# Gate products two iterations sooner, three pieces taken tile by tile, sums of squares on GpSimd

## What is computed

```python
for i in range(2):
    h = rmsnorm(x, g0) * (1 + scale) + shift
    y = short_conv_mixer(h) if i == 0 else ssd_mixer(h)
    x = x + gate * rmsnorm(y, g1)
    h = rmsnorm(x, g2) * (1 + scale) + shift
    x = x + gate * rmsnorm(swiglu_ffn(h), g3)
```

## Time and profile before

| what | value |
|---|---|
| median of 3 runs | 3520.47 us (3519.66 to 3521.72) |
| the profiled execution: its time, its span | 3519.32 us, 3517.4 us |
| mean granted TensorE clock | 0.950 of full speed |
| busy, share of the span | PE 86%, DVE 61%, ACT 40%, POOL 17% |
| HBM traffic over the span | 226 GB/s |

### The profile page before, as it was taken

How to read it: one execution, slowest core, us unless ns; L and a number is a source line. 1 busy time by engine, 2 the same in 40 slices (tenths; PEclk the granted TensorE clock), 3 DMA queues, 4 the chain that set the end, 5 groups by cost and what they waited for, 6 DMA issues and landing times.

```text
span 3517.4 us, 34727 instructions
## 1 busy us (share of the span) xinstructions
PE 3008.4 (86%) x12066; PEld 2079.7 (59%) x12066; DVE 2138.0 (61%) x3994; ACT 1399.4 (40%) x2882; POOL 599.3 (17%) x540
## 2 busy tenths in 40 slices
PE   5999999799777889999888978987879787777777
PEld 4867888587555668888667864465546432223222
DVE  6655443677555544443255479988777979755555
ACT  3233222344444542222472245775434333333333
POOL 0000000000000000000000003334444354443442
PEclk9999999899888999999999989999989999999999
DMA  6544444244111324443220449898999999999998
GB/s 222 181 143 126 144 141 136 76 142 128 37 36 36 102 81 147 140 149 118 97 90 13 166 178 350 302 357 347 407 420 419 355 414 421 421 421 421 421 421 345
DMA packets 147549, 797.84 MB, mean 227 GB/s; under 512 B 16304, under 2 KB 18480, under 8 KB 81712
## 3 DMA queue, kind: packets, MB, share of 16 engines
q0 software_dynamic: 73728, 536.90, 37.6%
q1 hardware_dynamic: 69840, 251.69, 22.0%
q10 hardware_dynamic: 3808, 7.02, 0.6%
HBM read 793.46 MB, written 2.10 MB: 226 GB/s over the span
## 4 chain that ended last, share of the span: by engine, by line
PE 52%; DMA 19%; DVE 19%; ACT 6%; issue 3%; POOL 0%; DVEq 0%; SPq 0%; ACTq 0%; POOLq 0%
PE psum L153 52%; DMA tail<-in_experts,tail 19%; DVE tail L187 4%; DVE tail L170 2%; ACT L164 2%; DVE arena L182 2%; ACT arena L164 2%; DVE tail L182 2%; DVE tail L193 1%; DVE tail L190 1%; DVE region L170 1%; ACT tail L164 1%; DVE tail L196 1%; DVE tail L205 1%; DVE arena L170 1%
## 5 line engine op out<-in xcount | busy, mean ns | idle before, releaser
L153 PE MATMUL psum<-tail,arena 128*128 128x256 f32 (+2 forms) x3580 | 1267.3, 503 | 266.5 <-ACT arena L164 236.2
L153 PE MATMUL psum<-rounded,rounded 128*128 128x512 f32 x5496 | 1321.0, 401 | 99.9 <-ACT arena L164 58.4
L153 PEld LDWEIGHTS psum<-rounded,rounded 128*128 128x128 f32 x5496 | 1051.1, 193 | 345.5 <-ACT arena L164 61.4
L153 PEld LDWEIGHTS psum<-tail,arena 128*128 128x128 f32 x3580 | 674.2, 198 | 813.8 <-issue 756.7
L216 POOL DMA_INDIRECT tail<-in_experts,tail x512 | 581.5, 1136 | 1760.9 <-DVE tail L199 864.6
L187 DVE CUSTOM_DVE_ANT_0 tail<-tail 128x1024 f32<-128x1024 f32 x512 | 621.1, 1224 | 307.0 <-DMA tail<-in_experts,tail 305.5
L164 ACT ACTIVATE tail<-tail 128x1 f32<-128x1 f32 (+1 forms) x1056 | 266.4, 252 | 780.0 <-DVE tail L187 742.6
L170 DVE TENSOR_TENSOR rounded<-arena,rounded 128x1024 fp32r<-128x1024 f32 (+2 forms) x285 | 316.5, 1111 | 364.6 <-ACT rounded L164 364.4
L164 ACT ACTIVATE rounded<-arena 128x1024 fp32r<-128x1024 f32 (+2 forms) x317 | 291.7, 939 | 446.2 <-DVE arena L170 238.9
L153 PE MATMUL psum<-arena 128*128 128x1 f32 (+3 forms) x792 | 201.1, 378 | 77.3 <-ACT arena L164 37.6
L164 ACT ACTIVATE arena<-psum 128x256 f32<-128x256 f32 (+2 forms) x210 | 97.6, 481 | 407.2 <-PE psum L153 406.4
(11 more groups left out here) (82 smaller groups left out, 1483.9 us busy)
## 6 DMA issues: line engine op xcount, KB each, us to landing
arena<-in_ada SPq DMA_DIRECT2D x136, 512.0 KB, 3.9
arena<-in_fin SPq DMA_DIRECT2D x88, 512.0 KB, 4.2
arena<-in_win SPq DMA_DIRECT2D x56, 512.0 KB, 3.3
arena<-in_fout SPq DMA_DIRECT2D x32, 512.0 KB, 4.0
...
```

The costliest lines, as they stand in the source:

```text
L153: return self.e.matmul(o, a, b, start=start, stop=stop, skip_group_check=skip)
```

## The change

- **Mixer's loop**: z(kk) goes to TensorE in iterations 2kk+3 and 2kk+4, still ahead of part b; ACT's silu stands in iteration 2kk+4, after `act_ssd_b` and before part a; DVE's gate multiplication in 2kk+5, with a wait on its own skip term. The norm of group g moves from n = 4g+10 to n = 4g+8, its TensorE sum behind part b. Tiles 0 to 7 of the output are rounded in iterations 32 and 33, and only half a z piece is left after the loop.
- **Norms**: scaling and EPS go into ACT's Ln, which reads PSUM (`dve_rstd` goes, all over the kernel); the delta rule's q and k keep an addition on DVE.
- **Sums of squares**: `pool_out` adds the squares of tiles 0 to 6 on GpSimd into `ysum`, and TensorE does 2 sums per layer in place of 8; `pool_pair_sum` adds a group's two tiles, 1 sum in place of 2.
- **Boundaries**: the gain is applied in ACT's copy of y; DVE multiplies and adds in place. A third piece is prepared in `act_pre`/`dve_pre` (layers 1 to 3), and `pe_first` takes three pieces (two in layer 0) tile by tile, the third four tiles behind.
- **Step sizes**: DVE does one operation of the softplus per projection; the turning and the sums move from projection 4 and 6 to 24 and 26.

```diff
-def dve_rstd(e, name, last, n, r, width=512):
+def act_rstd(e, name, last, n, r, width=512):
...
-    e.ts(r, ps[name][:, 0:width], 1.0 / n, ALU.mult, EPS, ALU.add).then_inc(*ps.release(name))
-def act_rstd(e, name, r):
+    e.act(r, ps[name][:, 0:width], ACT.Ln, bias=cc("eps"), scale=1.0 / n).then_inc(*ps.release(name))
...
-    e.act(r, r, ACT.Ln).then_inc(*ln_ok.tick(name))
-    e.wait_ge(*ln_ok.at(name))
...
 def pe_pre(e, i):
...
 def act_pre(e, i):
+    if i:
+        act_ahead(e)
...
-    act_rstd(e, ("pre", i), rst[0])
+    act_rstd(e, ("pre", i), ("pre", i, 7), D, rst[0])
...
 def dve_pre(e, i):
-    dve_rstd(e, ("pre", i), ("pre", i, 7), D, rst[0])
+    if i:
+        dve_ahead(e)
...
+def pe_first(e, i, keys):
+    own = [ps.claim(key, ALL) for key in keys]
+    for k in range(8 + 4 * (len(keys) - 2)):
+        for u, key in enumerate(keys):
+            m = k - 4 if u == 2 else k
+            if 0 <= m < 8:
+                if m == 0:
+                    e.wait_ge(*ps.vacant(key))
+                pe_gemm(e, pc[key], own[u], hrhs, ready=h_at(i), own=[m])
+    for key in keys:
+        pe_after(e, pc[key], ALL)
 def pe_out(e, i, groups, rhs, ready, norm=True, behind_first=None):
...
-        if norm and kk:
-            pe_stat(e, ("post", i, kk - 1), stat, ones, kk == 1, False)
...
+        e.wait_ge(*sq.done(("post", i, 6)))
+        e.mm(stat, ones, ysum, True, False)
...
 def act_out(e, i, groups):
...
-        act_square(e, ("post", i, kk), ps["y", i, kk])
-        e.act(yT[:, kk, :], ps["y", i, kk], ACT.Copy).then_inc(*ps.release(("y", i, kk)))
-    act_rstd(e, ("post", i), rst[1])
+        if kk:
+            act_square(e, ("post", i, kk), ps["y", i, kk])
+        else:
+            e.act(ysum, ps["y", i, kk], ACT.Square).then_inc(*sq_ok.tick(("post", i, kk)))
+        if kk < 7:
+            act_y(e, i, kk)
+    act_rstd(e, ("post", i), ("post", i, 7), D, rst[1])
+    act_y(e, i, 7)
+def act_y(e, i, kk):
+    e.wait_ge(*der_ok.at((i, "post")))
+    e.act(yT[:, kk, :], ps["y", i, kk], ACT.Copy, scale=post(i, kk)).then_inc(*ps.release(("y", i, kk)))
...
 def dve_out(e, i, groups):
+    dve_derived_post(e, i)
...
-    dve_derived_post(e, i)
-    dve_rstd(e, ("post", i), ("post", i, 7), D, rst[1])
+    e.wait_ge(*rs_ok.at(("post", i)))
...
-            if k == 0:
-                e.wait_ge(*der_ok.at((i, "post")))
-                e.wait_ge(*rs_ok.at(("post", i)))
-            if k > 1:
-                e.wait_ge(*x_ok.at((i, k - 2)))
-            e.stt(gd[k % 2], yT[:, k, :], post(i, k), rst[1], ALU.mult, ALU.mult).then_inc(
-                *dve_b.tick(("post", i, k)))
+            e.wait_ge(*ps.done(("y", i, k)))
+            e.tt(yT[:, k, :], yT[:, k, :], rst[1], ALU.mult).then_inc(*y_sc.tick((i, k)))
...
-            e.wait_ge(*dve_b.at(("post", i, k - 1)))
-            e.tt(xT[:, k - 1, :], xT[:, k - 1, :], gd[(k - 1) % 2], ALU.add).then_inc(
-                *x_ok.tick((i, k - 1)))
+            e.wait_ge(*y_sc.at((i, k - 1)))
+            e.tt(xT[:, k - 1, :], xT[:, k - 1, :], yT[:, k - 1, :], ALU.add).then_inc(*x_ok.tick((i, k - 1)))
+def pool_out(e, i):
+    for kk in range(1, 7):
+        key = "post", i, kk
+        e.wait_ge(*sq_ok.at(key))
+        if kk > 1:
+            e.wait_ge(*sq.done(("post", i, kk - 1)))
+        e.tt(ysum, ysum, sq[key], ALU.add).then_inc(*sq.release(key))
...
 def pe_ffn(e, half):
-    for kk in range(KF):
-        for part in range(2):
+    pe_first(e, half, [("ffn", half, 0, 0), ("ffn", half, 0, 1), ("ffn", half, 1, 0)])
+    for kk in range(1, KF):
+        for part in range(1 if kk == 1 else 0, 2):
...
-            pe_gemm(e, pc[key], o, hrhs, ready=h_at(half) if kk == 0 and part == 0 else None)
+            pe_gemm(e, pc[key], o, hrhs)
...
 def act_ffn(e, half):
...
-        act_ahead(e)
+        if kk:
+            act_ahead(e)
...
-def pe_dt(e):
-    p = pc["dt"]
-    o = ps.claim("dt", ALL)
-    e.wait_ge(*ps.vacant("dt"))
-    pe_gemm(e, p, o, hrhs, ready=h_at(2))
-    pe_after(e, p, ALL)
-def softplus_dve(e, x, tmp3, ok, sig, tag):
+def softplus_steps(e, x, tmp3, ok, sig, tag):
...
     done(e.ts(u, w, 2.0, ALU.add))
+    yield
     done(e.recip(u, u))
+    yield
...
+def softplus_dve(e, x, tmp3, ok, sig, tag):
+    for _ in softplus_steps(e, x, tmp3, ok, sig, tag):
+        pass
 def act_dt(e):
-    act_ahead(e)
...
 def dve_dt(e):
-    dve_ahead(e)
...
-    softplus_dve(e, dtT, [a[0:32, :] for a in sp], dt_act.at("exp"), dt_dve, "dt")
+    yield from softplus_steps(e, dtT, [a[0:32, :] for a in sp], dt_act.at("exp"), dt_dve, "dt")
+    yield
...
+    yield
...
 def pe_xbc(e):
-    for n in range(32):
-        if n == 4:
+    pe_first(e, 2, ["dt", ("xbc", 0), ("xbc", 1)])
+    for n in range(2, 32):
+        if n == 24:
...
-        if n == 6:
+        if n == 26:
...
 def act_xbc(e):
...
-        if n == 4:
+        if n == 24:
...
-        if n == 6:
+        if n == 26:
...
 def dve_xbc(e):
+    steps = dve_dt(e)
...
+        next(steps, None)
...
 def pool_ssd(e):
-    for n in range(32):
-        g, c = ITS[n]
+    for n in range(33):
+        if norm_of(n) is not None:
+            pool_pair_sum(e, norm_of(n))
+        g, c = ITS[n] if n < 32 else (0, 3)
...
+    pool_pair_sum(e, 7)
...
 def pe_ssd_b(e, n):
...
 def pe_norm_pair(e, g, banks):
...
-    for u in range(2):
-        pe_stat(e, ("zn", g, u), o, ones, u == 0, u == 1)
+    e.wait_ge(*sq.done(("zn", g, 0)))
+    pe_stat(e, ("zn", g, 1), o, ones, True, True)
+def pool_pair_sum(e, g):
+    e.wait_ge(*sq_ok.at(("zn", g, 1)))
+    e.tt(sq["zn", g, 1], sq["zn", g, 1], sq["zn", g, 0], ALU.add).then_inc(*sq.release(("zn", g, 0)))
...
 def act_pair_squares(e, g):
...
 def dve_z(e, kk):
...
+    e.wait_ge(*ps.done(("sy", kk // 2, kk % 2)))
...
-def dve_pair_rstd(e, g):
-    dve_rstd(e, ("zn", g), ("zn", g, 1), 256, rst[g % 2])
...
-second_of = lambda n: (n - 6) // 2 if n > 5 and n % 2 == 0 else None
-silu_of = lambda n: (n - 7) // 2 if n > 6 and n % 2 else None
-norm_of = lambda n: (n - 6) // 4 - 1 if n > 9 and n % 4 == 2 else None
+second_of = lambda n: (n - 4) // 2 if n > 3 and n % 2 == 0 else None
+gate_of = lambda n: (n - 5) // 2 if n > 4 and n % 2 else None
+norm_of = lambda n: (n - 8) // 4 if n > 7 and n % 4 == 0 else None
...
+round_of = lambda n: range(4 * (n - 32), 4 * (n - 31)) if n >= 32 else ()
...
 def pe_ssd(e):
...
-        if n > 4:
-            pe_z(e, (n - 5) // 2, FRONT if n % 2 else BACK)
+        if n > 2:
+            pe_z(e, (n - 3) // 2, FRONT if n % 2 else BACK)
+        if n > 1:
+            pe_ssd_b(e, n - 2)
...
-        if n > 1:
-            pe_ssd_b(e, n - 2)
...
-    pe_z(e, 14, BACK)
-    pe_norm_pair(e, 6, RG)
-    pe_after(e, pc["z", 14], RG)
-    pe_z(e, 15, range(8))
+    pe_z(e, 15, BACK)
...
 def act_ssd(e):
...
-        if silu_of(n) is not None:
-            act_z(e, silu_of(n))
+        if second_of(n) is not None:
+            act_z(e, second_of(n))
...
-            act_rstd(e, ("zn", norm_of(n)), rst[norm_of(n) % 2])
+            act_rstd(e, ("zn", norm_of(n)), ("zn", norm_of(n), 1), 256, rst[norm_of(n) % 2])
...
+        act_o(e, round_of(n))
+    act_z(e, 15)
...
-    act_z(e, 14)
-    act_pair_squares(e, 6)
-    act_o(e, range(0, 4))
-    act_rstd(e, ("zn", 6), rst[0])
-    act_ahead(e)
-    act_z(e, 15)
+    act_o(e, range(8, 10))
...
-    act_o(e, range(4, 10))
-    act_rstd(e, ("zn", 7), rst[1])
-    act_o(e, range(10, 16))
+    act_o(e, range(10, 14))
+    act_rstd(e, ("zn", 7), ("zn", 7, 1), 256, rst[1])
+    act_o(e, range(14, 16))
...
 def dve_ssd(e):
...
-        if silu_of(n) is not None:
-            dve_z(e, silu_of(n))
-        if norm_of(n) is not None:
-            dve_pair_rstd(e, norm_of(n))
+        if gate_of(n) is not None:
+            dve_z(e, gate_of(n))
...
+        dve_o(e, round_of(n))
+    dve_z(e, 15)
...
-    dve_z(e, 14)
-    dve_pair_rstd(e, 6)
-    dve_o(e, range(0, 4))
-    dve_after(e, pc["z", 14])
-    dve_norm_pair(e, 6)
-    dve_ahead(e)
-    dve_z(e, 15)
...
-    dve_o(e, range(4, 10))
-    dve_pair_rstd(e, 7)
-    dve_o(e, range(10, 12))
+    dve_o(e, range(8, 14))
...
-    dve_o(e, range(12, 16))
+    dve_o(e, range(14, 16))
...
 def act_o(e, tiles_of):
...
+        e.wait_ge(*s_pe.at(31))
+        e.wait_ge(*s_ce.at(31))
...
 def dve_o(e, tiles_of):
...
-            act_rstd(e, ("rn", f, n // 2), rst[n // 2 % 2])
-        yield
-def dve_qkv(e, f):
-    for s in range(15):
-        n = s - 3
-        if 0 <= n < 8 and n % 2:
...
-            dve_rstd(e, ("rn", f, g), ("rn", f, g), 64, rst[g % 2])
+            act_rstd(e, ("rn", f, g), ("rn", f, g), 64, rst[g % 2])
+        yield
+def dve_qkv(e, f):
+    for s in range(15):
...
-            dve_rstd(e, ("dnn", f, g), ("dnn", f, g), 1.0, R4[g])
+            e.wait_ge(*sq.done(("dnn", f, g)))
+            e.ts(R4[g], ps["dnn", f, g], EPS, ALU.add).then_inc(*ps.release(("dnn", f, g)))
...
-    for g in range(2):
-        act_rstd(e, ("dm", f, g), rst[g])
```

(14 more changed lines are left out.)

48 lines of the change are left out of this document (27 added, 21 removed).

## The result

The changed kernel takes **3441.22 us** (median of 4 runs, 3437.34 to 3443.28), the kernel before 3520.06 beside it: ratio 0.9774, 95% interval 0.9757 to 0.9791. The forecast was 3438.0 in 3400 to 3476. Four or five runs of one kernel lie up to 12 us apart (3437.0 to 3448.7 in the widest case), so a difference of a few us between two medians is only used where a trace shows its place.

The account below looks back on a forecast made before the run. TensorE was taken as full in the projections, the mixer's loop as bound by waits between engines. Savings of 21.9, 5.8, 2.0, 3.5, 7.6, 32 and 8 sum to 81 us; 3519.3 less 81 gives 3438, range 3400 to 3476.

Parts of the forecast that it names:

- 1, sums: Output stages: six fewer TensorE sums of squares per layer at 0.91 us each, 21.9 us saved in four layers.
- 2 and 3, norms, x update, pieces: Layer boundaries and norms: shorter norm chains save 5.8 us, x update 2.0, three pieces tile by tile 3.5 (0 to 10).
- for the last stage itself I count nothing: Last stage: fewer DVE instructions, a few more ACT waits; no gain counted, bounded by 5 us either way.
- 4, step sizes: Projections: one step-size operation per projection; the third projection's 7.07 us wait shrinks; 7.6 us saved (4 to 11).
- 5, the loop: Mixer's loop: period falls from 41.0 to 35.5 us, 32 saved over six periods (18 to 45), 8 after the loop.
- The pair's sum: Mixer's loop: GpSimd's sum of a pair ends after part b's start, costing 0.4 us per period, inside TensorE's idling.
- A: Mixer's loop: all eight periods stay near 41 us, as ACT's queue and a low clock return the gain; 3470; chance 0.21.
- B: Mixer's loop becomes bound by TensorE, 27 to 29 us per period; 3393 us; chance 0.12.
- C: Output stages and norms: GpSimd's adds make it slower, 3563 us at 12 us per add; chance 0.05, other losses included.
- D: Whole kernel: nothing moves, the first block's gain is taken back before the gathers; 3519 us; chance 0.02.
- E: Mixer's loop: a further 1.3 us drain per ACT table load, 45 us in all; 3483 us; chance 0.01.
- The rule on VectorE and GpSimd: Mixer's loop: whichever starts first blocks the other; pair sum could hold DVE 1 to 2 us per period, some 11.

Follow-up runs that it names:

- both-first: Changed kernel with ACT, in the loop's even iterations, rounding the next state at the head and taking the gate's silu ahead of state copy and Exps: 3410.58 us.
- the runs with the rounding first: Changed kernel with ACT rounding the next position's state at the head of the loop's even iterations: 3421.53 us alone, 3410.58 with silu ahead, 3425.74 with silu last.

## Why the prediction was right, step by step

The range and the mechanisms held. That the total came within 3 us (78.8 measured, 81 in the sum) is partly luck: the sums gave 3 us less than forecast, the loop's end 2 less, norms with x update and pieces 5 more, step sizes 1 more, the loop up to S(32) 3 more, and the stages behind 1706 us took back 6.4 that weren't in the sum.

- **1, sums:** 21.9 forecast, 18.5 measured. GpSimd's adds of 1.3 us are hidden, as said. The price of a sum, 0.91 us from the difference of two pacings, was a little high: 6.32 - 5.45 = 0.87 where it stands, which with six per layer is 5.2. From first product to last sums the layers gained 4.0, 5.8, 4.8 (layer 2, from S(32)) and 4.0; why less than 5.2 in three of them isn't placed.
- **2 and 3, norms, x update, pieces:** 11.3 forecast. What the ledger leaves at the attention's first product is 84.3 - 18.6 (sums) - 8.6 (step sizes: 27.0 - 18.4) - 35.0 (S(2) to S(32)) - 6 = 16. Of these, 11.2 lie at the boundaries, where norms and x update work: layer 0's first product comes 2.2 sooner, and from the last sums of a layer to the next first product it is 1.6, 1.7, 2.6 and 3.1 us less (24.81 to 23.20, 23.10 and 22.24; 23.10 to 19.98 ahead of the attention). The forecast for them was 7.8. The form of the norm was put back at one boundary only, the last, and cost 0.3 us there. The other 4.9 lie inside the layers (2.0, 1.1 and 1.9 in layers 0, 1 and 3) and aren't placed. The step of part 3 that failed is the 3.5 us left after its own deductions: they were too small, and in layer 2 the later end of the step sizes' product makes a loss of it, 1.65 us.
- **What stands behind the layers**, inside part 2 and "for the last stage itself I count nothing": failed, and by the prediction's own sign. It was to be wrong if the stages after 1706 us were longer or shorter by more than the bound of 5; from the attention's first product to the end they took 1810.9 us and take 1817.3, 6.4 more. I counted 1.6 us of gain for four short chains and missed an owner: a bank that DVE had freed at once is now freed by ACT, late in its queue. By the medians the new form of these norms cost 6.7 us; by the trace 4.1 behind the first gather (1516.1 less 1512.0) and 1.0 ahead of it. Some 1 of the 1.9 us that the attention stage lost stays unexplained.
- **4, step sizes:** 7.6 forecast, 8.6 in the ledger, 6.7 in the run; waits 1.37 and 1.05 for 1.7 and 1.4. The credit for the pieces within it (1.5) was wrong in sign (-1.65).
- **5, the loop:** forecast 11.9, 7.65, 9.3, 5.9; measured 11.07, 7.75, 9.07, 5.90. Six periods 32 forecast, 37.2 in the ledger, 36.7 by two runs that differ in the order alone. By its own periods the sum would have 6 x 5.5 = 33 where it has 32. What was high is n%4 = 0. Its beginning lost 2.2 us where I had none. End of the loop: 8 forecast, 6 to 7 measured.
- **The pair's sum:** 0.4 us per period forecast, nothing measured in this order, where TensorE idles anyway. In the order of before it cost 14 us.
- **Rivals.** A is out: no period stays near 41. B did not happen, but the runs that reorder ACT's queue show that much of it was to be had: both-first takes 30.2 us per period (181.07/6) against B's 27 to 29 and the 34.6 of the changed kernel. C is out by one number, 1.30 us for a 128x512 add, against the 9 us from which it decides. D and E are out.
- **The rule on VectorE and GpSimd** (the Trainium skill, "SBUF — State Buffer", section "Who interferes with whom"): the slowed pairs are still there, a multiplication on DVE takes 1.10 us beside one of GpSimd of 0.99. The 11 us that the rule would give for the pair's sum are not in the time (207.81 and 208.38 us with and without it), but that doesn't test the rule: in five of the seven periods from iteration 8 on GpSimd's add ends 0.1 us or more before DVE's next operation (996.05 + 1.28, then 997.42), so the two hardly meet. In the runs with the rounding first they do, and DVE's 128x256 operation takes 0.80 us in place of 0.43. Behind the loop one engine is held for the other too, as the rule says, but the add through six operations of DVE and not through one (4.79 us).
- **The drain behind a table load** (the Trainium skill, "ScalarE: Activation LUTs", section "What ACT_TABLE_LOAD costs"): not seen after the change either. The load at 238.17 lasts 1.28 us and the Exp starts at 239.47.
